# Attention of a five-layer kernel: two query tiles share one mix of 256 columns, and the softmax divide moves behind it

## What is computed

```
logits = einsum('bqkgd,bjkd->bkgqj', q_b, k_b) * scale
p = sink_softmax(where(mask, logits, NEG_INF), sink_l)      # e / (sum(e) + exp(sink - m))
o = einsum('bkgqj,bjkd->bqkgd', p, v_b)
y_l = (o * silu(z_l)) @ w_out
```

## Time and profile before

| what | us |
|---|---|
| median of 3 runs (2427.62 to 2429.78) | 2429.62 |
| profiled execution | 2425.73 |
| its span, first to last instruction | 2423.9 |
| TensorE busy with products | 2286.8 (94%) |
| VectorE busy | 1227.8 (51%) |
| ScalarE busy | 640.7 (26%) |
| mean DMA rate over the span | 234 GB/s |

### The profile page before, as it was taken

One profiled execution on the slowest core, in us unless ns is written; L12 is line 12 of the kernel. 1 busy time (PEld: TensorE's weight loads), 2 busy tenths in 40 slices (PEclk: granted clock), 3 DMA queues, 4 the chain that ended last, 5 costly groups with the idle time before them and its releaser, 6 DMA issues. The chain is left out here.

```text
span 2423.9 us, 30405 instructions
## 1 busy us (share of the span) xinstructions
PE 2286.8 (94%) x10828; PEld 1236.2 (51%) x10829; DVE 1227.8 (51%) x2803; ACT 640.7 (26%) x1470; POOL 36.7 (2%) x47
## 2 busy tenths in 40 slices
PE   7999899999999997988999799999999999999997
PEld 3545586478745566775886663333323323333332
DVE  3868558453892584568454444333433334333433
ACT  3017542343210254317331421111111111111111
POOL 0000000000000000000001000000000000000000
PEclk9999999999999999999999899999999999999999
DMA  9630034301564101671241169989999998998998
GB/s 375 217 139 31 1 140 174 112 1 36 178 226 152 36 1 70 219 267 36 70 157 52 49 268 401 417 352 420 421 391 391 421 422 358 421 421 358 422 422 331
DMA packets 139562, 568.21 MB, mean 234 GB/s; under 512 B 11824, under 2 KB 13872, under 8 KB 90064
## 3 DMA queue, kind: packets, MB, share of 16 engines
q1 hardware_dynamic: 139472, 567.01, 59.3%
HBM read 565.93 MB, written 1.05 MB: 234 GB/s over the span
## 5 line engine op out<-in xcount | busy, mean ns | idle before, releaser
L2925 PE MATMUL PS<-BIG,PW 128*64 128x512 f32 x2304 | 512.7, 595 | 24.3 <-DMA BIG<-in_w 23.8
L2925 PEld LDWEIGHTS PS<-BIG,PW 128*64 128x64 f32 x2304 | 159.9, 137 | 367.5 <-issue 293.0
L3166 DVE TENSOR_SCALAR PW<-PS 128x512 f32<-128x512 f32 x36 | 24.9, 692 | 484.5 <-PE PS L2925 484.5
L2964 PE MATMUL PS<-BIG,PW 128*64 128x512 f32 x1152 | 255.4, 595 | 8.6 <-ACT PW L2799 8.6
L338 DVE SCALAR_TENSOR_TENSOR PW<-BIG,COND,PW 128x512 f32<-128x512 f32 x352 | 236.9, 747 | 0.6
L2796 ACT ACTIVATE PW<-PW 128x512 f32<-128x512 f32 x36 | 22.7, 630 | 732.4 <-DVE PW L3166 732.4
L2964 PEld LDWEIGHTS PS<-BIG,PW 128*64 128x64 f32 x1152 | 79.1, 137 | 161.1 <-issue 144.0
L1173 PE MATMUL PS<-HT,BIG 128*128 128x512 f32 (+1 forms) x448 | 155.2, 502 | 0.0
L1173 PEld LDWEIGHTS PS<-HT,BIG 128*128 128x128 f32 x448 | 84.6, 190 | 62.8 <-issue 56.7
L703 PE MATMUL PS<-HT,BIG 128*128 128x256 f32 x512 | 111.6, 379 | 1.4 <-PEq L908 1.4
L1582 PE MATMUL PS<-BIG,HT 128*128 128x512 f32 x256 | 111.6, 594 | 0.0
(11 more groups left out here) (529 smaller groups left out, 3194.1 us busy)
## 6 DMA issues: line engine op xcount, KB each, us to landing
BIG<-in_w SPq DMA_DIRECT2D x384, 1024.0 KB, 16.8
BIG<-in_l_w_in SPq DMA_DIRECT2D x20, 2048.0 KB, 8.4
BIG<-in_l_w_ada SPq DMA_DIRECT2D x40, 1024.0 KB, 7.5
BIG<-in_w_ada SPq DMA_DIRECT2D x24, 1024.0 KB, 7.4
BIG<-in_l_w_out SPq DMA_DIRECT2D x8, 2048.0 KB, 8.0
BIG<-in_w_in SPq DMA_DIRECT2D x7, 2048.0 KB, 8.1
BIG<-in_l_w_ada SPq DMA_DIRECT2D x4, 2048.0 KB, 15.7
BIG<-in_w_out SPq DMA_DIRECT2D x2, 2048.0 KB, 7.7
```

What stands on the lines that cost most here:

```text
L2925: ins = nc.tensor.matmul(PS[64 * g:64 * g + 64, 4 + half, :], xt[:, c % 4, c // 4, :], W[:, c, half * F + g * 512:half * F + g * 512 + 512 ...
L2964: ins = nc.tensor.matmul(PS[64 * g:64 * g + 64, 7, :], at_[:, k % 4, k // 4, :], W[:, 8 + k // 2, k % 2 * D + g * 512:k % 2 * D + g * 512 ...
```

## The change

`attention` is rewritten around couples of units (2c, 2c+1).

- Mix: one product of a head and key tile takes both query tiles, 256 columns. `turned` is laid out for a couple, in two buffers; the second is new space (`spare`). Key tiles that only the second query tile sees (dilated attention) are mixed for it alone, 128 columns.
- Order: a couple's mix is split into two halves, for two turns, and comes 2 + `lag` turns behind (lag 1, in the dilated attention 0): in turn i the half number i - 2 - lag. Inside the turn the half stands in groups (window and dilated: the two heads of a key tile; latent: one product) between the transposes of unit i. With four key tiles in both, that is 2 transposes, group, 3 transposes, group, 3 transposes.
- Divide: in all but the latent layer (`late`) the transposes take the exponentials undivided. Once for each couple VectorE adds the sinks' exponentials, takes the reciprocal and copies it out 64 wide (`invert`), TensorE transposes that in two transposes into the free half of the output's bank (`ready_to_mix`), and the gate multiplies it in as one operation more (`weighed`). The latent layer divides as before.
- The exponentials of the sinks are one instruction for each couple, from a shift that VectorE computes (`shifted`).
- VectorE's gates are one for each couple, 256 columns, placed two to four turns after the unit, behind the maxima.
- The unused interleaving of modulation steps (`mods`) goes.

The core of the diff (`turned` and the small tiles in front, the bookkeeping of semaphores behind and the layers' `value` and `gate`, which widen from P to LAT columns, are left out):

```
-        def attention(units, scale, score, value, mask_of, sink, gate, together=True, mods=None, parts=1):
+        def attention(units, scale, score, value, mask_of, sink, gate, spare, together=True, late=True, parts=1, lag=1):
...
+            turned = [x.rearrange("p (h j q s) -> p h j q s", h=2, j=4, q=2) for x in (PW[:, 2048:4096], spare[:, 0:2048])]
...
+            def halves(c):
+                order = [(j, h) for j in range(len(units[2 * c + 1][2])) for h in range(2)]
+                if not together:
+                    order.sort(key=lambda x: x[1])
+                return order[:len(order) // 2], order[len(order) // 2:]
...
+                    def turn_rows(i, rows):
+                        kts = units[i][2]
+                        for h, j in rows:
+                            if j == 0:
+                                pe.wait_ge(*at("scores_used" if late else "probs_ready", 2 * i + h + 1))
+                                if i >= 1:
+                                    pe.wait_ge(*at("turned_copied", 2 * i + h - 1))
+                            ins = nc.tensor.transpose(PS[:, 4 + h, j * P:(j + 1) * P], probs[:, i % 2, h, kts[j] * P:(kts[j] + 1) * P], ident)
+                            if j == len(kts) - 1:
+                                ins.then_inc(S["probs_turned"].sem, 1)
+
+                    def ready_to_mix(c):
+                        if c >= 2:
+                            pe.wait_ge(*at("heads_taken", c - 1))
+                        if late:
+                            pe.wait_ge(*at("inverse_ready", c + 1))
+                            for q in range(2):
+                                nc.tensor.transpose(scale_of(c)[:, q * P:(q + 1) * P],
+                                                    inverse_of(c)[:, q, :, :].rearrange("p h d -> p (h d)"), ident)
+                        pe.wait_ge(*at("turned_copied", 4 * c + 4))
+
+                    def mix_groups(c, half):
+                        both, kts = len(units[2 * c][2]), units[2 * c + 1][2]
+                        order = halves(c)[half]
+                        width = 2 if together else 1
+                        for x in range(0, len(order), width):
+                            for j, h in order[x:x + width]:
+                                lhs, place = value(units[2 * c], h, kts[j])
+                                q = 0 if j < both else 1
+                                ins = nc.tensor.matmul(place(heads_of(c))[:, q * P:], lhs, turned[c % 2][:, h, j, q:2, :],
+                                                       start=(j == 0), stop=(j == len(kts) - 1))
+                            if half == 1 and x + width >= len(order):
+                                ins.then_inc(S["heads_ready"].sem, 1)
+                            yield
...
                     def turn(i):
...
+                        part = i - 2 - lag
+                        if part < 0:
+                            turn_rows(i, rows)
+                            return
+                        c, half = part // 2, part % 2
+                        groups = len(halves(c)[half]) // (2 if together else 1)
+                        cuts = [x * len(rows) // (groups + 1) for x in range(groups + 2)]
+                        turn_rows(i, rows[:cuts[1]])
+                        if half == 0:
+                            ready_to_mix(c)
+                        for x, _ in enumerate(mix_groups(c, half)):
+                            turn_rows(i, rows[cuts[x + 1]:cuts[x + 2]])
...
                     for i in range(N):
                         if i + 2 < N:
                             scores(i + 2)
-                        modulate(i, 0)
                         turn(i)
-                        if i >= 1:
-                            mix(i - 1)
-                        modulate(i, 1)
-                    mix(N - 1)
+                    for part in range(N - 2 - lag, N):
+                        mix(part)
...
+                    def sink_exps(c):
+                        act.wait_ge(*at("a_ready", c + 1))
+                        nc.scalar.activation(es[:, c % 2, :, :], shifted[:, c % 2, :, :], ACT.Exp).then_inc(S["exp_ready"].sem, 1)
...
+                    def invert(c):
+                        dve.wait_ge(*at("scores_used", 4 * c + 4))
+                        d = den[:, c % 2, :, :]
+                        if sinks:
+                            dve.wait_ge(*at("exp_ready", c + 1))
+                            dve_chain.link(dve, nc.vector.tensor_tensor(d, d, es[:, c % 2, :, :], ALU.add))
+                        r = rd[:, c % 2, :, :]
+                        dve_chain.link(dve, nc.vector.reciprocal(r, d))
+                        nc.vector.tensor_copy(inverse_of(c), r.unsqueeze(3).to_broadcast([P, 2, 2, 64])).then_inc(S["inverse_ready"].sem, 1)
...
+                    def gates(c):
+                        dve.wait_ge(*at("heads_ready", c + 1))
+                        o, z, src = gate(units[2 * c], heads_of(c))
+                        if late:
+                            w = weighed[:, c % 2, :]
+                            dve_chain.link(dve, nc.vector.tensor_copy(w, scale_of(c)) if z is None else
+                                           nc.vector.tensor_tensor(w, scale_of(c), z, ALU.mult))
+                            z = w
+                        nc.vector.tensor_tensor(o, src, z, ALU.mult).then_inc(S["heads_taken"].sem, 1)
...
                     for i in range(N):
-                        normalise(i)
-                        modulate(i, 0)
+                        if not late:
+                            normalise(i)
                         if i + 2 < N:
                             maxima(i + 2)
-                        if i >= 1:
-                            gates(i - 1)
-                        modulate(i, 1)
-                    gates(N - 1)
+                        if late and i % 2 == 1:
+                            invert(i // 2)
+                        if i >= 4 + lag and (i - lag) % 2 == 0:
+                            gates((i - 4 - lag) // 2)
+                    for c in range((N - 3 - lag) // 2, couples):
+                        gates(c)
```

More of the change, by code:

```diff
@@ L935, in mix @@
-                    def mix(i):
-                        pe.wait_ge(*at("turned_copied", 2 * i + 2))
-                        if i >= (1 if mods else 2):
-                            pe.wait_ge(*at("heads_taken", i if mods else i - 1))
-                        kts = units[i][2]
-                        order = [(j, h) for j in range(len(kts)) for h in range(2)]
-                        if not together:
-                            order.sort(key=lambda x: x[1])
-                        for j, h in order:
-                            lhs, place = value(units[i], h, kts[j])
-                            ins = nc.tensor.matmul(place(heads_at(i)), lhs, turned[:, i % 2, h, j * P:(j + 1) * P],
-                                                   start=(j == 0), stop=(j == len(kts) - 1))
-                        ins.then_inc(S["heads_ready"].sem, 1)
@@ new lines, in mix @@
+                    def mix(part):
+                        if part % 2 == 0:
+                            ready_to_mix(part // 2)
+                        for _ in mix_groups(part // 2, part % 2):
+                            pass
+                    def turn(i):
+                        rows = [(h, j) for h in range(2) for j in range(len(units[i][2]))]
+                        part = i - 2 - lag
[10 more added lines that the diff above has]
+                            turn_rows(i, rows[cuts[x + 1]:cuts[x + 2]])
@@ L1027, in normalise @@
                         dve.wait_ge(*at("scores_used", 2 * i + 2))
[L1028 to L1032 removed]
+                        d, r = den[:, i // 2 % 2, i % 2, :], rd[:, i // 2 % 2, i % 2, :]
@@ L1046, in modulate @@
-                    def modulate(i, late):
-                        for step, j in steps[2 * i + late]:
-                            if step == "take":
-                                mods.take(dve, j)
-                    if sink is not None:
+                            nc.vector.tensor_scalar(pr, pr, r[:, h:h + 1], None, ALU.mult).then_inc(S["probs_ready"].sem, 1)
+                    def gates(c):
[7 more added lines that the diff above has]
+                        nc.vector.tensor_tensor(o, src, z, ALU.mult).then_inc(S["heads_taken"].sem, 1)
@@ L1267, in masked @@
                 return (x, window[:, u[1], x:x + P]) if u[1] < 2 else None
-            attention(units, 64 ** -0.5, score, value, masked, bcast(f"l{i}_sink"), gate)
+            attention(units, 64 ** -0.5, score, value, masked, bcast(f"l{i}_sink"), gate, a.take(3072))
             if need_ctx:
```

118 lines of the change are left out of this document (48 added, 70 removed).

## The result

The changed kernel takes 2434.59 us (median of 12 runs, 2431.23 to 2440.12). The kernel before, run in turn with it, takes 2428.74 us (12 runs, 2423.66 to 2436.0). The ratio is 1.0028 with a 95% interval of 1.0019 to 1.0038: slower by about 6 us, a little more than the 0.2% that I called no change.

A forecast was written before the change was run, and what follows sets the result against it. VectorE bound long turns by a hair (TensorE 3.11 us of work in 3.30). Stages -0.1, +3.65, -2.0 and -1.0 sum to +0.55 us on 2429.62: 2430.1 us; own range 2426 to 2434.5, outer 2415 to 2438.

The forecast's parts named there:

- way out in full: Rival, chance 0.12: leaving column tiles for transposes costs 0.12 us more at each of some 70 places, 8.5 us; 2438 us.
- Price of a change of form: TensorE: each change between full array, row tiles and column tiles costs 0.15 us, whatever the semaphores.
- Free groups: Rival, chance 0.22 (or half free): TensorE moves between column tiles and transposes without paying, -15 us; 2415 us.
- 70 places: Count of places where TensorE leaves column tiles for transposes; 0.20 us at each was set as deciding, total past +4.9.
- The long turn: Window-layer turn with four key tiles: 3.65 us, TensorE now the bound, against 3.30 before, +0.35 us.
- The short turn: Window-layer turn with two key tiles: 2.06 us against 2.34 before, -0.28 us.
- the short turns keep their latency: Rival, chance 0.09: copies, exponentials or scores' bank become the loop, the short turns' 3.1 us are not gained; 2433 us.
- The start: First window layer: first mix comes two turns later, so scores 5 start 1.35 us earlier.
- The end of the first window layer: Leftover mixes fill old waits, -0.8 us; last gate's second operation +0.6; no wait put in front of others.
- The latent layer: Streaming -0.6 us, last two units' waits for the divide -1.7 of 1.96, last gate +0.3; sum -2.0 us.
- The last window layer: 16 long tiles: start -1.4 us, 11 turns +3.85, end +0.6, last gate +0.6; sum +3.65 us.
- The dilated stage: Divide and its wait leave, two multiplies and twelve changes of form a couple (1.8 us) come in; sum -1.0 us.

The follow-up runs named there:

- e10: Changed kernel with the dilated attention's exponentials divided ahead of the transposes, no inverse and a plain copy as gate; 2431.36 us (one run).
- e11: The changed kernel once more, unaltered, for a second profile; 2439.63 us (one run).
- e2: Changed kernel with each half mix as one group in the middle of the transposes; 2424.59 us, ratio 0.9984 to the kernel before.
- e3: Kernel before with only its 128-column mix, one turn behind, cut into groups between the transposes; 2438.07 us, ratio 1.0050 to the kernel before.
- e6: Changed kernel, groups kept, with the dilated attention's mix one turn later; 2431.47 us, ratio 1.0015 to the kernel before.
- e5: Changed kernel with the dilated attention done as in the kernel before; 2432.59 us, ratio 1.0025 to the kernel before.

## Why the prediction was right, and where it was not

The forecast was 2430.1 us in a range of 2415 to 2438, most likely within 0.2% of before. The time, 2434.6, is in the range, and 4.5 us above the forecast. In part that is luck. The forecast's own range ended at 2434.5; the outer range holds the time with room only because of *way out in full*, which the runs rule out. And the kernel before, at 2429.62 when I forecast, has a median of 2428.74 in the runs beside the changed one, which hides 0.9 us: as a difference I forecast +0.55 and the medians give +5.85. So the time is on the slower side of the bound that I drew, for a reason that none of my rivals names.

- **Price of a change of form: right.** 0.15 us was argued from the earlier trace rows. The turns with no, one and two groups (3.21, 3.36, 3.66) show it, each as forecast from it. *Free groups* is out, and so is *way out in full*: that would have made the long turn 3.9 us, and it is 3.66. (My mark for deciding it, 0.20 us a place with a total of +4.9, does not fit my own 70 places: 0.05 more at each gives +4.05.)
- **The long turn: right.** 3.65 forecast, 3.66 measured; a group 0.58, as said; no wait of TensorE. VectorE's list fits as well: the broadcast copy is 0.29 (0.25 estimated), the wide multiplies 0.42, and a couple keeps it for 5.4 us of the 7.3, all but its two waits (2.7 a turn, 2.8 forecast).
- **The short turn: right.** 2.06 forecast and measured, so *the short turns keep their latency* is out.
- **The start: a little better.** Scores 5 start at 201.49, before at 203.46: 2.0 earlier, with 1.35 forecast.
- **The end of the first window layer: worse.** The leftover mixes fill the old waits, but a new one of 0.67 us for a copy comes in, which I had ruled out ("No wait is put in front of others"); the timeline below shows it, and the ends of the latent and the last window layer have one like it (0.34 and 0.35). No turn in the middle has one. The block behind starts after 1.25 us of idle time where it was 0.66, the +0.6 forecast for the gate's second multiply. The stage is +0.3 instead of -0.1.
- **The latent layer: right in kind, too high.** The last two units should have lost nearly all of their waits. TensorE's timeline at its end, below, shows what is left: the divide there still costs 0.60, and the next unit waits 0.34 for a copy; of 1.96 us 1.0 is gained, not 1.7. The block behind starts after 1.05 us (0.78 before). -1.3 instead of -2.0.
- **The last window layer: right.** +3.65 forecast, +3.8 at the same clock.
- **The dilated stage: the step that failed.** -1.0 forecast, +3.3 measured, which is 4.3 of the 5.3 us by which the difference is off. My terms there do not show how they come to -1.0, and one is miscounted: I charged twelve changes of form a couple (1.8 us), and the trace has eight, two more than before. Corrected alone, that would have put the forecast lower and the miss higher. What failed is the clock: I priced the changes at the 0.15 us of full clock, although shows this stage at a granted clock of 0.64, and I took that clock as given, the same for both kernels. It was not: with the new order of work it is 0.53. The table of low levels shows the clock held down wherever groups stand in the stage with the mix close behind. The late divide and its inverse are 1.2 of the 3.3 us (e10).

The ends of the first window layer's and the latent layer's attention in the changed kernel, TensorE, against the earlier trace rows:

```profile
281.25 0.41 PE L947 MATMUL PS<-CONST,PW 128*128 128x128 f32 x2 [0.67 <-ACT BIG L1027]
...
539.68 0.33 PE L947 MATMUL PS<-CONST,PW 128*128 128x128 f32 x1 [0.60 <-DVE PW L1079]
...
541.54 0.30 PE L947 MATMUL PS<-CONST,PW 128*128 128x128 f32 x1 [0.34 <-ACT BIG L1027]
...
546.74 5.63 PE L703 MATMUL PS<-HT,BIG 128*128 128x256 f32 x25 [1.05 <-PEq L923]
```

**What stays open.** Why the clock stays at the low level is not settled. That the low level makes the stage long is shown by TensorE's busy time; that the groups together with the close mix keep it low is a pattern over thirteen profiles, and no run tells how. The runs show with which orders it stays: in all five profiles of groups with the mix close behind (changed, e11, e2, e10, e3) it lasts 23.9 to 34.1 us; in the one with groups and the mix later it lasts 13.7; and without groups, 13.7 to 20.5, sometimes with 6.8 more. It is not idleness of TensorE alone: the changed kernel has the busier TensorE there (23.5 of 26.5 us, against 18.2 of 23.2 before), though slower work is also longer busy. The single profile of e6 is thin for the other side, and its gain over the changed kernel (3.1 us of medians, intervals of the ratios overlapping) is smaller than the stage's 4.5. In e5 too the median gives back less than the profile (2.0 for 3.3).

The page "TensorEngine Tiling (Array Packing)" of the Trainium skill, section Tiling Modes, says that a change of tiling mode drains the engine. Every turn here agrees, at 0.15 us each at full clock. The page "TensorE: Matmul & The Clock Gate" of the Trainium skill (Part 2) says that the engine can pull weight loads ahead of running matmuls. Across a change of form the changed kernel does not show it, as the trace of before did not: at 281.81 us the first weight load of a group and its first product start together.

## What to carry to other kernels

Count the changes of the array's form in a turn before you interleave small products with full-array ones: at 0.15 us each, two groups among eight transposes cost 0.45 us, more than the 0.09 us that the later divide had freed in a long turn (3.30 to 3.21). Where an engine is freed from a divide or another hot operation, gather the work on TensorE by form (here a couple's whole mix in every second turn), and do not spend the room on interleaving. A stage whose granted clock is low has to be priced at that clock and at the other, since a new order of work can change which one it gets.

## What the runs showed of the hardware

- A change between full array, row tiles and column tiles costs 0.15 us at full clock: 3.21, 3.36 and 3.66 us for a turn with three, four and six. The way from column tiles back to transposes, which no row of before showed, costs what the others do: with two groups a turn has six changes for three, and takes 0.45 us more. I had not expected it to hold to a hundredth.
- With two column tiles at once, 8 products of 256 columns take as long as 16 of 128: 1.01 against 1.02 us. The width saves nothing where streaming sets the pace.
- A stage of 24 to 27 us with TensorE busy nine tenths of it (23.5 of 26.5 us) stayed at 1.2 GHz nearly throughout in both profiles of the changed kernel, while the same work with its mix one turn later rose to 2.4 GHz after 13.7 us. I had not expected the order of the same products to do that.
